# The order of VectorE's spectrum units in a long-convolution stage on one Trainium2 core

## The reference, cut to what matters

```python
def fft_long_conv(z, kfull):
    L = z.shape[1]
    zf = jnp.fft.rfft(z, n=2 * L, axis=1)
    kf = jnp.fft.rfft(kfull, n=2 * L, axis=0)
    return jnp.fft.irfft(zf * kf[None], n=2 * L, axis=1)[:, :L]

def hyena_mixer(u, conv_w, conv_b, w1, b1, w2, b2, w3, freq, skip):
    L = u.shape[1]
    uc = short_conv3(u, conv_w, conv_b)
    v, x1, x2 = jnp.split(uc, HY_ORDER + 1, axis=-1)
    k = hyena_filters(L, w1, b1, w2, b2, w3, freq)
    z = v.astype(jnp.float32)
    for o, gate_o in enumerate((x1, x2)):
        z = gate_o.astype(jnp.float32) * (fft_long_conv(z, k[:, o]) + skip[o].astype(jnp.float32) * z)
    return z.astype(u.dtype)
```

## Time and profile before

| what | value |
|---|---|
| time, median of 3 runs | 4545.72 us |
| lowest and highest | 4545.66 and 4546.92 us |
| the profiled execution's own time | 4546.92 us |
| its span in the profile | 4545.1 us |
| TensorE matmuls (PE) busy | 4212.6 us, 93% of the span |
| VectorE (DVE) busy | 1910.9 us, 42% |
| GpSimd (POOL) busy | 1406.1 us, 31% |
| ScalarE (ACT) busy | 1231.5 us, 27% |
| mean granted TensorE clock | 0.969 of full |

### The profile page before, as it was taken

How to read it: one execution, slowest core, us unless ns; L and a number is a source line. 1 busy time by engine, 2 the same in 40 slices (tenths; PEclk the granted TensorE clock), 3 DMA queues, 4 the chain that set the end, 5 groups by cost and what they waited for, 6 DMA issues and landing times.

```text
span 4545.1 us, 49646 instructions
## 1 busy us (share of the span) xinstructions
PE 4212.6 (93%) x19244; PEld 2998.0 (66%) x19244; DVE 1910.9 (42%) x2169; ACT 1231.5 (27%) x1869; POOL 1406.1 (31%) x974
## 2 busy tenths in 40 slices
PE   7999998899999998856999999998999989999997
PEld 3644775345655565355888888886666668888886
DVE  2252662304666675384154314323344456323322
ACT  3111331212221221212133223224444444223222
POOL 1110000001011111872234454443444444444443
PEclk8999999999999999978999999999999999999999
DMA  5110003300000001162122232232000022223232
GB/s 207 47 33 24 0 0 141 123 24 20 20 24 20 24 14 61 47 109 61 48 91 92 97 102 92 97 102 93 24 19 24 24 80 94 96 97 102 94 100 102
DMA packets 107396, 303.06 MB, mean 67 GB/s; under 512 B 16868, under 2 KB 34559, under 8 KB 106928
## 3 DMA queue, kind: packets, MB, share of 16 engines
q1 hardware_dynamic: 94752, 264.14, 18.5%
q0 software_dynamic: 5024, 22.63, 1.3%
q10 hardware_dynamic: 7472, 14.22, 0.8%
HBM read 277.62 MB, written 20.97 MB: 66 GB/s over the span
## 4 chain that ended last, share of the span: by engine, by line
PE 60%; issue 17%; POOL 11%; DVE 8%; ACT 2%; DMA 1%; POOLq 0%; ACTq 0%; DVEq 0%; SPq 0%
PE banks L270 21%; PE banks L284 15%; PE banks L2667 6%; POOL w_parts L255 6%; PE banks L1323 3%; PE banks L823 3%; PE banks L1350 2%; PE banks L2741 2%; DVE neg_max L902 2%; PE banks L2770 1%; PE banks L2757 1%; PE banks L1304 1%; PE banks L640 1%; DVE arena L1590 1%; DMA w_ring<-in_weights 1%
## 5 line engine op out<-in xcount | busy, mean ns | idle before, releaser
L255 POOL TENSOR_TENSOR w_parts<-w_ring,w_parts 128x1024 fp32r<-128x1024 f32 x344 | 835.7, 2430 | 1125.5 <-ACT w_parts L248 1125.5
L270 PE MATMUL banks<-x_high,w_parts 128*128 128x512 f32 x2944 | 911.7, 390 | 0.0
L284 PE MATMUL banks<-hidden,w_ring 128*128 128x512 f32 x1728 | 772.7, 602 | 36.4 <-DMA w_ring<-in_weights 19.8
L248 ACT ACTIVATE w_parts<-w_ring 128x1024 fp32r<-128x1024 f32 x344 | 364.5, 1060 | 1290.6 <-PE banks L270 1283.7
L270 PEld LDWEIGHTS banks<-x_high,w_parts 128*128 128x128 f32 x2944 | 552.6, 188 | 116.8 <-issue 2.1
L284 PEld LDWEIGHTS banks<-hidden,w_ring 128*128 128x128 f32 x1728 | 326.3, 192 | 448.1 <-issue 426.1
L270 PE MATMUL banks<-x_low,w_parts 128*128 128x512 f32 x1472 | 572.7, 389 | 0.0
L270 PE MATMUL banks<-hidden_high,w_parts 128*128 128x512 f32 x1600 | 482.1, 391 | 6.0 <-POOL w_parts L255 6.0
L2875 DVE TENSOR_TENSOR_SCAN arena<-arena,flags 128x128 f32<-128x128 f32 (+3 forms) x192 | 229.5, 1200 | 287.4 <-ACT arena L2816 286.0
L270 PEld LDWEIGHTS banks<-hidden_high,w_parts 128*128 128x128 f32 x1600 | 301.9, 189 | 71.1 <-POOL w_parts L255 6.8
L270 PEld LDWEIGHTS banks<-x_low,w_parts 128*128 128x128 f32 x1472 | 276.3, 188 | 59.1 <-issue 1.9
(11 more groups left out here) (387 smaller groups left out, 5416.4 us busy)
## 6 DMA issues: line engine op xcount, KB each, us to landing
w_ring<-in_weights SPq DMA_DIRECT2D x460, 512.0 KB, 3.4
resid<-in_xT ACTq DMA_DIRECT2D x2, 2048.0 KB, 26.2
arena<-in_fn_seq POOLq DMA_DIRECT2D x1, 4096.0 KB, 16.7
resid_spill<-resid POOLq DMA_DIRECT2D x1, 4096.0 KB, 12.3
hidden<-resid_spill POOLq DMA_DIRECT2D x1, 4096.0 KB, 13.9
s_in<-hidden SPq DMA_DIRECT2D x4, 1024.0 KB, 8.9
hidden<-s_in SPq DMA_DIRECT2D x32, 128.0 KB, 5.6
hidden<-s_out SPq DMA_DIRECT2D x4, 1024.0 KB, 4.8
```

The lines of the kernel that those rows point to most:

```text
L248: nc.scalar.activation(WP[:, g % 2, 0, :], WR[:, (g % RING) * TILE:(g % RING + 1) * TILE], ACT.Identity).then_inc(w_hi, 1)
L255: nc.gpsimd.tensor_tensor(WP[:, g % 2, 1, :], WR[:, (g % RING) * TILE:(g % RING + 1) * TILE], WP[:, g % 2, 0, :].bitcast(F32), ALU.subtrac ...
L270: mm = nc.tensor.matmul(PS[:, bank + h // H, :], w[a][:, k % KB, :], srcs[b][:, k, at + h:at + h + H], start=(first and i + q == 0), stop= ...
L284: mm = nc.tensor.matmul(PS[:, b + h // H, 0:w], W[:, s, k, :], src[:, k, h:h + w], start=(k == 0), stop=(k == KB - 1))
```

## The change

In every round VectorE now does all four `z_unit`s first, waits for them (`sp_d`), and then does spectrum(n, 0), conv(at[0]) and spectrum(n, 1). Before, it did `z_unit` 0 and 1, spectrum(n, 0), `z_unit` 2 and 3, conv(at[0]) and spectrum(n, 1).

```diff
             for n in range(6):
                 at = tiles_at(n)
-                for mb in range(2):
-                    for u in (2 * mb, 2 * mb + 1):
-                        z_unit(n, u)
-                    v.wait_ge(sp_d, 10 * n + 8 + 2 * mb)
-                    if mb and n < 5:
-                        conv(at[0])
-                    spectrum(n, mb)
+                for u in range(4):
+                    z_unit(n, u)
+                v.wait_ge(sp_d, 10 * n + 10)
+                spectrum(n, 0)
+                if n < 5:
+                    conv(at[0])
+                spectrum(n, 1)
                 if n < 5:
                     conv(at[1])
                 gated(n)
```

## The result

The changed kernel takes 4569.56 us (median of 5 runs, 4567.9 to 4571.06), the kernel before in the same comparison 4546.28 us: a ratio of 1.0051, 95% interval 1.0036 to 1.0065, 23.3 us slower. Forecast were 4565.9 us and 20.2 us. The profiled execution took 4570.35 us with a span of 4568.5; before it was 4545.1.

The account below looks back on a forecast made before the run. TensorE was taken as the bound, pausing for VectorE before each round's first inverse. 16.8 us of shift plus 3.4 us of clock made 20.2 us, so 4567.1 us profiled or 4565.9 as a median; stated range 4557 to 4575.

Parts of the forecast that it names:

- What bounds it: Hyena stage: TensorE, busy 93% of the span, waits 15.4 us in six first inverses for VectorE, whose order sets the pauses' end.
- The two waits for the copies: VectorE before z_unit 2 and 3: stands 2.17 and 2.16 us for ScalarE's copies, 4.33 us now empty.
- larger shift of 3.22 us: Rounds 2 and 4: inverse(n,0) 3.22 us later, against 2.60 in the other four, since GpSimd lost only 0.5 us there.
- `z_unit` 3 not stopped by GpSimd: Lines 1572 and 1573 during GpSimd's multiplication: one SBUF operand each, so no hold-up taken, 0 us.
- the spectrum's first instruction stopped: Line 1577 of spectrum(n,0), two SBUF operands: stands until GpSimd is done, about 3 us (0.69 + 2.3) once a round.
- Rival 2: The lock also catches z_unit 3: 1.33 us more a round, 8.0 in six, 4573.9 us; chance 0.08.
- GpSimd alone takes 4.5 us: GpSimd's multiplication, line 1275, with nobody ahead of it: 4.5 us, ends 4.38 and 4.89.
- 19.18 us from GpSimd's start to the inverse: Each round: 4.35 + 14.73 + 0.10 us to inverse(n,0), before 16.58 or 15.96; costs 16.8 us (16.1 to 19.2).
- Rival 1: Nothing measurable: VectorE slips in ahead of GpSimd, no spectrum is stopped; 2.2 us later, 4547.9 (4551.3 with the clock); chance 0.08.
- Nothing is given back: Rest of each round and the output stage: later work moves with inverse(n,0), so TensorE recovers none of the shift.
- The clock: TensorE at 1.2 GHz behind longer pauses: falls also in rounds 0 and 4, 2 x 1.7 = 3.4 us.
- Rival 3: Faster: later stretches are spared clock falls, 1.7 us each; 18 spared on balance give 4535.3 us; chance 0.02.

Follow-up runs that it names:

- experiment 2: Kernel before, old order kept, with GpSimd's multiplication waiting for the end of spectrum(n, 1): 4523.26 us, ratio 0.9949.
- Experiment 4: Kernel before, with z_unit 2 and 3 placed inside spectrum(n,0), where VectorE need not wait for their copies: 4545.33 us, ratio 1.0002.
- experiment 5: Changed kernel with GpSimd's multiplication cut in two, the even half starting at the end of TensorE's unit 2: 4549.47 us, ratio 1.0010 to the kernel before.
- experiment 1: Changed kernel with GpSimd's multiplication waiting for the end of spectrum(n, 1): 4550.71 us, ratio 1.0011 to the kernel before.
- Experiment 8: Kernel before with the changed order in one round only: round 5 alone 4549.27 us, ratio 1.0007; round 0 alone 4549.35 us, ratio 1.0009.
- experiment 6: Changed kernel with extra matmul calls before inverse(n,0) in rounds 0 to 4: ten calls 4569.33 us, five calls 4554.84 us.

## Why the prediction was right

- **What bounds it**: TensorE waits for VectorE at inverse(n,0). Confirmed by the waits after, and by experiment 2, in which the waits and 22.7 us go.
- **The two waits for the copies, 2.17 and 2.16 us**: measured 2.17 and 2.16 in rounds 0, 1, 3 and 5; in rounds 2 and 4 the first is 2.8, which is where the forecast's larger shift of 3.22 us there comes from. Experiment 4 shows that they are the cost: the same units, without a wait, cost nothing.
- **`z_unit` 3 not stopped by GpSimd, the spectrum's first instruction stopped**: 0.69, 0.68 and 3.17 us. Rival 2, 8 us more, falls; experiment 5 shows the same for `z_unit` 2. The Trainium skill's page SBUF — State Buffer (§ Who interferes with whom) says that two SBUF inputs contend with GpSimd's reads and one does not; the trace agrees on both counts, by these three numbers.
- **GpSimd alone takes 4.5 us**: measured 4.51 to 4.53. The Trainium skill's GPSIMD Engine Reference (§ 3.1, Elementwise) gives 4497 ns for an addition of this size, not for "exactly this operation" as the prediction has it; the trace agrees within 0.7% for the multiplication.
- **19.18 us from GpSimd's start to the inverse, 16.8 us in six rounds**: measured 19.16 to 19.17 and 16.7. Rival 1, no conflict in the changed order, is what experiment 1 makes by hand: 16.7 us and 4550.7, so its price was also right, but the chip does not do it by itself.
- **Nothing is given back**: the stage grows by 23.5 us and the program by 23.4. Experiment 8 agrees: with round 5 alone changed, its 2.6 us of shift arrive at the output stage (2.7 measured).
- **The clock, 3.4 us with ends of -5.1 and +3.8**: mis-sized, and outside its upper end. The six falls that I forecast came, but in rounds 0, 2 and 4 they took 9.9 to 10.2 us for the inverse instead of the 8.8 taken from the rows: 6.6 us in all. I had argued from one long pause (5.84 us, 8.96 us) that a longer pause costs no more. Behind pauses of 5.5 us the inverses took between 8.6 and 9.9 us, so one row was no bound. This term is nearly all of the 3.1 us by which the difference was missed.

Rival 3, many falls spared elsewhere, did not come: outside the stage the traces differ by 1.7 us.

## What to carry to other kernels

Before moving an instruction ahead of others on its engine, look up when its input arrives: the engine stands still for all that is missing, and work that filled that time is pushed behind it. An instruction much longer than its twins of the same shape, with another engine's long instruction beside it, marks a conflict to look at before the order around it: here, moving GpSimd's one multiplication behind the second spectrum brought 22.7 us where reordering VectorE lost 23.3. Reckon a wait of TensorE with the slower matmuls behind it, and take that price from several rows, since it scatters.

## What the runs showed of the hardware that I had not expected

Behind pauses of equal length (5.51 and 5.52 us) the same 32 records took 8.60, 8.73, 9.74, 9.86 and 9.92 us in one trace. The granted clock (third number from the right) of the changed kernel shows how. The rows are inverse(0,0) in two stretches of 4 us, and inverse(1,0) in one of 4 and one of 3.6:

```profile
1145.60:1149.60 4.00, 3.94 (x9) 3.20 (x10) 3.93 (x6) 0.00 (x0) 0.00 (x0) 0.50 0.02 4
1149.60:1153.60 4.00, 4.00 (x15) 3.28 (x14) 3.93 (x5) 0.00 (x0) 0.00 (x0) 0.72 0.00 0
...
1271.40:1275.40 4.00, 3.90 (x11) 3.20 (x12) 3.93 (x6) 0.00 (x0) 0.00 (x0) 0.59 0.01 4
1275.40:1279.00 3.60, 3.60 (x19) 3.16 (x18) 3.53 (x5) 0.00 (x0) 0.00 (x0) 1.00 0.00 0
```

In round 0 the clock stood at 1.2 GHz for the whole of the first 4 us and part of the next, in round 1 only for most of the first. Over all thirteen traces three groups show. Behind a pause of at most 1.76 us (five of these in experiment 6) no inverse was slow: 7.17 us, seven of seven. Behind 4.37 us or more all were: 8.60 to 10.19 us, 28 of 28. Between, from 1.98 to 3.35 us, 22 of 34 were slow, and the others took 7.14 or 7.17 us, even in the same round of the same code: 7.14 and 8.83 us in round 0 behind 1.98 and 1.99 us. Nor does the pause's length set the size. In experiment 1 a pause of 3.05 us stood before both of these:

```profile
1388.97 7.17 PE L1350 MATMUL banks<-arena 128*128 128x256 f32 x32 [3.05 <-DVE arena L1598]
...
1637.67 10.23 PE L1350 MATMUL banks<-arena 128*128 128x256 f32 x32 [3.05 <-DVE arena L1598]
```

What decides it stays open; it wasn't tried.
